# Axial attention with matmuls of 64 and 4 rows on different partitions, and softmax sums normalised inside it

## The chip, the cores and the metric

The kernel runs on one NeuronCore of a Trainium2 chip. The time is that of the whole program on the device, in microseconds (us). The core has a matrix engine (PE; its weight loads are listed apart as PEld), VectorE (DVE), ScalarE (ACT), GpSimd (POOL), and a queue, SP, from which all transfers of this kernel are issued.

## The reference

A trunk of two layers is applied with the same weights to a prompt of 1024 tokens and a sample of 512, all of width 1024. The first, even layer has eight heads of a dilated sliding window beside eight of a latent attention. The second, odd layer is the one that changes:

```
q = rms_norm(q.reshape(B, T, 16, 64), q_norm)        # 16 query heads
k = rms_norm(k.reshape(B, T, 4, 64), k_norm)         # 4 key heads, each for 4 query heads
q, k = axial rope of both (row angles, column angles)
s = einsum(q, k) * 64 ** -0.5                        # dense, per head, prompt and sample apart
p = softmax(s)
o = einsum(p, v)
y = (o * silu(gate)) @ w_out
return x + rms_norm(y, g_post)
```

## The kernel before

Everything is float32. A product of two float32 matrices is made of three matmuls on rounded parts ("hi", and the rest, "lo"): hi x hi, hi x lo, lo x hi. The program runs in phases with a barrier between them: `entry` (projections of layer 0), `attention` of its 16 heads, `output_projection`, `project` (projections of layer 1), `attention` again for the 16 axial heads (tag "c"), `output_projection`. Each engine has its own instruction list, written out in the code's order, and waits on semaphores.

`attention` goes through heads (NH = 16) and ten stages each (NS = 10), g = 10 h + s. Stages 0 and 1 take two of the sample's four key tiles each against its 512 queries, stages 2 to 9 one of the prompt's eight key tiles against 1024 queries. A tile is 128 keys; scores stand transposed, keys on partitions and queries in the free dimension. Per stage:

- PE, `scores` (L1444): for each half x of the score tile SA a matmul of KA (k hi on partitions 0 to 63, k lo on 64 to 127) with Q1 (q hi twice), and one of KB with Q3: 64 rows of k hi with q lo, and 8 rows of ones with rows that hold minus the maximum of each query. So the maximum is already subtracted. The second one has 72 rows.
- ACT: the exponential of SA into PF (L1550), its rounded part PH (L1553; in two stages of ten on DVE, L1657); POOL or DVE: PL = PF - PH (L1689, L1629).
- PE, `pv(g - 3)` (L1484, L1491): six matmuls with V as weights. VH has 64 columns of v and one of ones, so the 65th output row is the sum of the probabilities. They collect in OP (prompt) and OS (sample).
- PE, `max_unit` (L1374): two matmuls of 128 rows give q.k of 128 queries with 512 keys for the next head; DVE takes their maxima (L1601). Once for the sample and once for the prompt of each head a small matmul with the identity transposes the maxima (`transpose_max`, L1387), and DVE multiplies them with a table of minus ones into the rows of Q3 (`augment`, L1619).

After a head's last product ACT copies outputs and sums together (`evac_prompt`, `evac_sample`, L1534, L1543), and SP writes outputs to att_out, sums to att_den. `output_projection` reads the sums, inverts them on DVE (L1943), splits them (L1899, L1945), writes both parts to memory and reads them back as 32 rows (L1795 to L1810). Then per tile of 128 features and 512 tokens the PE spreads them with a matmul of 32 rows (L1864, into rb), DVE multiplies the outputs with it (L1953) and with the gate (L1956), ACT and DVE split them (L1909, L1939). The PE's products (L1877, 24 per output tile) of one third of the tokens run while the next third is prepared.

The score code of the kernel before, for an axial head:

```
for x in range(2):
    out = SA[:, x * CH:(x + 1) * CH]
    q0, k0 = (SEQ, SEQ + (2 * s + x) * P) if s < 2 else (x * CH, (s - 2) * P)
    qs, ks = slice(q0, q0 + CH), slice(k0, k0 + P)
    if stacked[h]:
        mms = [(ka[:, ks], q1[:, qs]), (kb[0:na, ks], q3[0:na, qs])]
    for i, (w, y) in enumerate(mms):
        mm = nc.tensor.matmul(out, w, y, start=(i == 0), stop=(i == len(mms) - 1))
```

## Time and profile before

| | |
|---|---|
| median of 3 runs | 2460.87 us (2458.8 to 2467.92) |
| the profiled execution, its own time | 2463.42 us |
| its span (first to last instruction) | 2461.6 us |
| mean granted TensorE clock | 0.928 of full speed |
| PE busy | 2148.5 us, 87% |
| DVE, POOL, ACT busy | 64%, 46%, 40% |

The span is the time between the first and the last instruction of the program; the execution's own time has a little more around it. A matmul's recorded length is modelled and overlaps with the next one's, so the distance between starts tells more than the length. L and a number is a line of the kernel before; a tile's name is without its buffer number (c_Q is Q1 or Q3).

### The profile page before, as it was taken

What the parts mean: (1) busy time and instruction counts of PE and PEld (TensorE: products, weight loads), DVE (VectorE), ACT (ScalarE), POOL (GpSimd) and SP (SyncE); (2) the same over time, 40 slices, a digit from 0 to 9 for tenths busy, and PEclk for the clock granted to TensorE, in tenths of its full rate; (3) what the DMA queues carried; (4) which work ended last, traced back from release to release, by engine and by line L of the source; (5) the groups of instructions that cost most, each with busy time, mean ns of one, the idle gap of its engine ahead of it and who ended that gap; (6) DMA issues with size and microseconds to landing.
All of it is one profiled execution on the core that took longest, in us unless ns stands there. A gap on an engine that the chain in (4) does not pass through costs nothing. (4 is left out here: it accounts for less than half of the span.)

```text
span 2461.6 us, 25658 instructions
## 1 busy us (share of the span) xinstructions
PE 2148.5 (87%) x9420; PEld 1600.6 (65%) x9420; DVE 1582.5 (64%) x1980; ACT 991.0 (40%) x1259; POOL 1124.1 (46%) x580
## 2 busy tenths in 40 slices
PE   6999988959999999958952987998699999996895
PEld 4777867847777766636742765787466666663674
DVE  7264156756776666625658999995377777773565
ACT  5132133213555566533323232210066666664331
POOL 5333443423555565523126767543266666663300
PEclk9999999977999999978976998999799999998898
DMA  4133487246555554244332222221623232313434
GB/s 154 35 118 129 128 295 192 73 118 126 116 117 112 115 114 99 59 133 140 99 106 83 78 94 98 82 94 65 149 50 82 65 75 65 73 39 112 157 103 128
DMA packets 223272, 262.75 MB, mean 107 GB/s; under 512 B 137440, under 2 KB 147040, under 8 KB 223152
## 3 DMA queue, kind: packets, MB, share of 16 engines
q1 hardware_dynamic: 223152, 261.17, 38.2%
q8 instruction: 72, 1.18, 0.2%
q14 instruction: 48, 0.39, 0.1%
HBM read 162.62 MB, written 98.50 MB: 106 GB/s over the span
## 5 line engine op out<-in xcount | busy, mean ns | idle before, releaser
L1689 POOL TENSOR_TENSOR c_PL<-c_PF,c_PH 128x1024 fp32r<-128x1024 f32 x128 | 307.0, 2399 | 199.1 <-ACT c_PH L1553 142.2
L1689 POOL TENSOR_TENSOR ab_PL<-ab_PF,ab_PH 128x1024 fp32r<-128x1024 f32 (+3 forms) x128 | 269.1, 2102 | 237.1 <-ACT ab_PH L1553 178.8
L1550 ACT ACTIVATE ab_PF<-ab_SA 128x1024 f32<-128x1024 f32 (+3 forms) x160 | 143.6, 897 | 243.6 <-PE ab_SA L1409 143.1
L1550 ACT ACTIVATE c_PF<-c_SA 128x1024 f32<-128x1024 f32 x160 | 164.3, 1027 | 168.7 <-PE c_SA L1444 168.7
L1601 DVE TENSOR_REDUCE c_MH<-c_SM 128x1 f32<-128x512 f32 x256 | 172.9, 688 | 85.2 <-PE c_SM L1374 83.6
L847 PE MATMUL e_acc<-e_XH,e_wh 128*128 128x512 f32 x480 | 197.8, 412 | 25.6 <-DVE e_XL_r L1016 16.1
L340 PE MATMUL p_acc<-XH,p_wh 128*128 128x512 f32 x432 | 186.4, 431 | 26.3 <-POOL Y_r L174 26.3
L847 PE MATMUL e_acc<-e_XL_r,e_wh 128*128 128x512 f32 x480 | 193.5, 403 | 0.0
L847 PE MATMUL e_acc<-e_XH,e_wl 128*128 128x512 f32 x480 | 193.4, 403 | 0.0
L340 PE MATMUL p_acc<-Y_r,p_wh 128*128 128x512 f32 x432 | 172.2, 399 | 0.0
L340 PE MATMUL p_acc<-XH,p_wl 128*128 128x512 f32 x432 | 172.1, 398 | 0.0
L1877 PE MATMUL o_acc<-o_XH,o_WH 128*128 128x512 f32 x384 | 156.6, 408 | 12.4 <-DVE Y_r L1939 12.4
L1877 PE MATMUL o_acc<-o_XH,o_WL_r 128*128 128x512 f32 x384 | 151.2, 394 | 0.0
L1374 PE MATMUL c_SM<-c_KA,c_Q 128*128 128x512 f32 x320 | 132.9, 423 | 20.0 <-DMA c_KA<-kC_lo 18.1
L1553 ACT ACTIVATE c_PH<-c_PF 128x1024 fp32r<-128x1024 f32 x128 | 135.7, 1060 | 4.1
L758 POOL TENSOR_TENSOR e_wl<-e_raw,e_wh 128x1024 fp32r<-128x1024 f32 (+1 forms) x31 | 72.9, 2353 | 135.0 <-ACT e_wh L910 135.0
L1601 DVE TENSOR_REDUCE ab_MH<-ab_SM 128x1 f32<-128x512 f32 x128 | 86.3, 688 | 68.9 <-PE ab_SM L1374 68.6
L1444 PE MATMUL c_SA<-c_Q,c_KA 128*128 128x512 f32 x320 | 127.2, 397 | 1.3 <-ACT c_PF L1550 1.3
L1444 PE MATMUL c_SA<-c_Q,c_KB 72*128 72x512 f32 x320 | 127.2, 398 | 0.0
L847 PEld LDWEIGHTS e_acc<-e_XH,e_wh 128*128 128x128 f32 x480 | 92.6, 193 | 53.3 <-POOL e_wl L758 24.6
L1592 DVE CUSTOM_DVE_ANT_0 ab_BS<-ab_SM,ab_Bhi 128x512 f32<-128x512 f32 (+1 forms) x192 | 83.0, 465 | 66.1 <-PE ab_SM L1370 65.4
L1553 ACT ACTIVATE ab_PH<-ab_PF 128x1024 fp32r<-128x1024 f32 (+3 forms) x128 | 119.6, 934 | 4.1
(255 smaller groups left out, 5569.9 us busy)
## 6 DMA issues: line engine op xcount, KB each, us to landing
o_G<-silu_gate SPq DMA_DIRECT2D x48, 256.0 KB, 2.8
c_Q<-qC_hi SPq DMA_DIRECT2D x32, 384.0 KB, 5.4
e_raw<-in_w_tiles SPq DMA_DIRECT2D x20, 512.0 KB, 3.8
p_raw<-in_w_tiles SPq DMA_DIRECT2D x18, 512.0 KB, 3.6
o_WL<-in_w_out SPq DMA_DIRECT2D x16, 512.0 KB, 5.6
e_XL<-in_xT SPq DMA_DIRECT2D x12, 512.0 KB, 9.8
silu_gate<-e_ta SPq DMA_DIRECT2D x24, 256.0 KB, 2.0
ab_Q<-qA_hi SPq DMA_DIRECT2D x16, 384.0 KB, 5.6
```

The costliest lines, as they stand in the source:

```text
L340: last_mm = nc.tensor.matmul(out, w[:, ks], x[:, k, cols(c)], start=(k == 0 and j == 0), stop=(k == KT - 1 and j == 2))
L758: nc.gpsimd.tensor_tensor(wl[w % 2][:, 0:width], raw[w % 2][:, 0:width], wh[w % 2][:, 0:width].bitcast(F32), ALU.subtract).then_inc(w_lo, 1)
L847: mm = nc.tensor.matmul(out, a[b][:, ks], x[:, k, cols(c)], start=(k + i == 0), stop=(k == KT - 1 and i == 2))
L1374: nc.tensor.matmul(SM[:, x * CH:(x + 1) * CH], Q1[h % 3][0:n, q0:q0 + P], keys(h)[0][0:n, k0:k0 + CH], start=True, stop=True).then_inc(m_r ...
L1444: mm = nc.tensor.matmul(out, w, y, start=(i == 0), stop=(i == len(mms) - 1))
L1550: nc.scalar.activation(used(PF[p], h, s), used(SA, h, s), ACT.Exp).then_inc(e_done, 1)
L1553: nc.scalar.activation(used(PH[p], h, s), used(PF[p], h, s), ACT.Copy).then_inc(p_hi[0], 1)
L1592: nc.vector.tensor_tensor_reduce(out=BS[:, x * CH:x * CH + n], in0=SM[:, x * CH:x * CH + n], in1=table.bitcast(F32), scale=1.0, scalar=-3. ...
L1601: nc.vector.reduce_max(dst, src, axis=AX_X).then_inc(m_done, 1)
L1689: nc.gpsimd.tensor_tensor(used(PL[p], h, s), used(PF[p], h, s), used(PH[p], h, s).bitcast(F32), ALU.subtract).then_inc(p_lo[0], 1)
L1877: mm = nc.tensor.matmul(acc[:, cols(n % NB)], w[:, t, ks], y, start=(k + j == 0), stop=(k == KT - 1 and j == 2))
```

## The change

The axial layer gets its own function `axial`; the even layer keeps `attention`. The order of work over heads and stages stays, with these differences:

- `scores`: KA with Q1 as before, for both halves. The low part of q is now a matmul of 64 rows, on partitions 0 to 63 for the first half and 64 to 127 for the second (KB holds k hi twice, Q3 the two halves of q lo one above the other). The maxima are subtracted by a matmul of their own, of 4 rows: ones on partitions 0 to 3 and, for the prompt's second half, 32 to 35.
- `max_unit` takes 64 rows: even units on partitions 64 to 127, odd ones on 0 to 63. One unit stands behind the scores, the other between the products with PH and those with PL.
- `pv`: VH has 64 columns of v and 64 of ones, so the sum stands in 64 output rows, above the output's partitions. The two VH matmuls come first, then the two with VL, which now has 64 columns.
- ACT makes 1/sum as exp(-ln(sum)) of those rows (`invert`), DVE multiplies the output with it (`normalise`). No sums are written; `output_projection` of layer 1 gets `raw=False` and leaves out everything on the sums, the 24 matmuls of L1864 and the multiplications of L1953. The one of layer 0 keeps them.

```

```diff
+def axial(nc, ar, A, S):
+    NH, NS, NU = 16, 10, 20
+    G = NH * NS
+    NP, NQ = SEQ // P, DEC // P
+    LAG = 3
+    SLOW_HI, SLOW_LO = (3, 5), (4, 8)
...
+        Q1 = [sc.sb(f"c_Q1{i}", [P, T], F32R) for i in range(3)]
+        KA = [sc.sb(f"c_KA{i}", [P, T], F32R) for i in range(2)]
+        KB = [sc.sb(f"c_KB{i}", [P, T], F32R) for i in range(2)]
+        Q3 = [sc.sb(f"c_Q3{i}", [P, 2 * CH], F32R) for i in range(2)]
+        AU = [sc.sb(f"c_AU{i}", [KR, 2 * CH], F32R) for i in range(2)]
+        VH = [sc.sb(f"c_VH{i}", [P, TT, 2 * HD], F32R) for i in range(2)]
+        VL = [sc.sb(f"c_VL{i}", [P, TT, HD], F32R) for i in range(2)]
...
+        RZ = [sc.sb(f"c_RZ{n}", [HD, w]) for n, w in (("s", DEC), ("p", SEQ))]
+        MH = sc.sb("c_MH", [P, NP, 2])
+        M = sc.sb("c_M", [P, 2 * R2 + NQ])
+        one = sc.sb("c_one", [KR, P], F32R)
...
+            def max_unit(h, u):
+                if u == 0:
+                    pe.wait_ge(in_q[h % 3], 32 * (h // 3 + 1))
+                    if h % 4 == 0:
+                        pe.wait_ge(in_k[h // 4 % 2], 32 * (h // 8 + 1))
+                wait_count(pe, m_done, NU * h + u - 1)
+                x, r = u % 2, rows(1 - u % 2)
+                q0, k0 = max_of(u)
+                nc.tensor.matmul(SM[:, half(x)], Q1[h % 3][r, q0:q0 + P], KB[h // 4 % 2][r, k0:k0 + CH],
+                                 start=True, stop=True).then_inc(m_ready, 1)
+            def transpose_max(h, prompt):
+                if prompt:
+                    pe.wait_ge(m_both, h + 1)
+                else:
+                    pe.wait_ge(m_done, NU * h + NQ)
+                wait_count(pe, aug_done, 2 * h + prompt)
+                src = M[:, 0:KR] if prompt else M[:, 2 * R2:2 * R2 + NQ]
+                nc.tensor.matmul(MT[0:KR if prompt else NQ, 0:P], src, ident[:], start=True, stop=True
+                                 ).then_inc(mt_ready, 1)
+            def scores(h, s):
+                q1, q3, au = Q1[h % 3], Q3[h % 2], AU[h % 2]
+                ka, kb = KA[h // 4 % 2], KB[h // 4 % 2]
+                if s == 0:
+                    pe.wait_ge(in_q3[h % 2], 64 * (h // 2 + 1))
+                    if h % 4 == 0:
+                        pe.wait_ge(in_kl[h // 4 % 2], 32 * (h // 8 + 1))
+                wait_count(pe, e_done, h * NS + s)
+                out = [SA[:, half(x)] for x in range(2)]
+                if s < 2:
+                    q0, k0, c, a = (SEQ, SEQ), (SEQ + 2 * s * P, SEQ + (2 * s + 1) * P), half(1), (0, 0)
+                else:
+                    q0, k0, c, a = (0, CH), ((s - 2) * P,) * 2, half(0), (0, R2)
+                for x in range(2):
+                    nc.tensor.matmul(out[x], ka[:, k0[x]:k0[x] + P], q1[:, q0[x]:q0[x] + CH], start=True, stop=False)
+                for x in range(2):
+                    nc.tensor.matmul(out[x], kb[rows(x), k0[x]:k0[x] + P], q3[rows(x), c], start=False, stop=False)
+                if s == 0:
+                    pe.wait_ge(aug_done, 2 * h + 1)
+                if s == 2:
+                    pe.wait_ge(aug_done, 2 * h + 2)
+                for x in range(2):
+                    r = slice(a[x], a[x] + 4)
+                    mm = nc.tensor.matmul(out[x], one[r, :], au[r, c], start=False, stop=True)
+                mm.then_inc(s_ready, 1)
+            def pv(g, between=()):
+                h, s = g // NS, g % NS
+                p, k = g % 4, h // 4
+                vh, vl = VH[k % 2], VL[k % 2]
+                if s == 0:
+                    if h % 4 == 0:
+                        pe.wait_ge(in_v[k % 2], 32 * (k // 2 + 1))
+                    wait_count(pe, o_out[0], h)
+                if s == 2:
+                    wait_count(pe, o_out[1], h)
+                def weighted(t, n, probs, first, last):
+                    for x in range(2):
+                        if s < 2:
+                            out, kt, st, en = OS[0:n, :], NP + 2 * s + x, s == 0 and x == 0, s == 1 and x == 1
+                        else:
+                            out, kt, st, en = OP[0:n, half(x)], s - 2, s == 2, s == NS - 1
+                        mm = nc.tensor.matmul(out, t[:, kt, 0:n], probs[:, half(x)], start=first and st, stop=last and en)
+                    return mm
+                on, n_hi = hi_at[g]
+                pe.wait_ge(p_hi[on], n_hi)
+                weighted(vh, P, PH[p], True, False)
+                weighted(vl, HD, PH[p], False, False)
+                for u in between:
+                    max_unit(h + 1 if s + LAG < NS else h + 2, u)
+                on, n_lo = lo_at[g]
+                pe.wait_ge(p_lo[on], n_lo)
+                weighted(vh, P, PL[p], False, True).then_inc(pv_done, 1)
...
+            for g in range(G):
+                h, s = g // NS, g % NS
+                units = range(2 * s, 2 * s + 2) if h + 1 < NH else ()
+                scores(h, s)
+                for u in units[:1]:
+                    max_unit(h + 1, u)
+                if s == 3 and h + 1 < NH:
+                    transpose_max(h + 1, 0)
+                if g >= LAG:
+                    pv(g - LAG, units[1:])
+                else:
+                    for u in units[1:]:
+                        max_unit(h + 1, u)
+                if s == 0:
+                    transpose_max(h, 1)
...
+            def invert(h, prompt):
+                act.wait_ge(pv_done, NS * h + (NS if prompt else 2))
+                wait_count(act, o_out[prompt], h)
+                src = OP[HD:P, :] if prompt else OS[HD:P, :]
+                nc.scalar.activation(RZ[prompt][:], src, ACT.Ln).then_inc(z_log[prompt], 1)
+                act.wait_ge(z_log[prompt], h + 1)
+                nc.scalar.activation(RZ[prompt][:], RZ[prompt][:], ACT.Exp, scale=-1.0).then_inc(z_inv[prompt], 1)
...
+                if s == 3 and h > 0:
+                    invert(h - 1, 1)
+                if s == 5:
+                    invert(h, 0)
...
+            def both(h):
+                dve.wait_ge(m_done, NU * (h + 1))
+                wait_count(dve, mt_ready, 2 * h)
+                out = M[:, 0:2 * R2].rearrange("p (a b) -> p a b", a=2)[:, :, 0:4]
+                lo, hi = (MH[:, :, j].rearrange("p (a b) -> p a b", a=2) for j in range(2))
+                nc.vector.tensor_tensor(out, lo, hi, ALU.max).then_inc(m_both, 1)
+            def augment(h, prompt):
+                dve.wait_ge(mt_ready, 2 * h + prompt + 1)
+                wait_count(dve, s_ready, NS * (h - 1))
+                n = KR if prompt else 4
+                out = AU[h % 2][0:n, half(1 - prompt)].rearrange("r (i n) -> r i n", n=P)
+                nc.vector.tensor_tensor(out, MT[0:n, 0:P].unsqueeze(1).to_broadcast([n, 4, P]), negsel[0:n, :, :],
+                                        ALU.mult).then_inc(aug_done, 1)
...
+            def normalise(h, prompt):
+                dve.wait_ge(z_inv[prompt], h + 1)
+                wait_count(dve, st[prompt][h % 2], 16 * (h // 2))
+                src = OP[0:HD, :] if prompt else OS[0:HD, :]
+                nc.vector.tensor_tensor(OB[prompt][h % 2][:], src, RZ[prompt][:], ALU.mult).then_inc(o_out[prompt], 1)
...
+                if s == 4 and h > 0:
+                    normalise(h - 1, 1)
+                if s == 6:
+                    normalise(h, 0)
...
+def output_projection(nc, ar, l, S, A, Y, rstd_next, gpost, ones, epst, xin, xout, raw):
...
-            sp.wait_ge(z_hi, 1)
-            sp.dma_start(flat(S["RZ", "hi"]), zh[:].bitcast(F32)).then_inc(z_out, 16)
-            sp.wait_ge(z_lo, 1)
-            sp.dma_start(flat(S["RZ", "lo"]), zl[:].bitcast(F32)).then_inc(z_out, 16)
+            if raw:
+                sp.wait_ge(z_hi, 1)
+                sp.dma_start(flat(S["RZ", "hi"]), zh[:].bitcast(F32)).then_inc(z_out, 16)
+                sp.wait_ge(z_lo, 1)
+                sp.dma_start(flat(S["RZ", "lo"]), zl[:].bitcast(F32)).then_inc(z_out, 16)
...
-            pe.wait_ge(rz_in, 32)
+            if raw:
+                pe.wait_ge(sel_set, 1)
+                pe.wait_ge(rz_in, 32)
             for period, t, g, a, p, x in stages():
-                if g is not None:
+                if g is not None and raw:
                     n = g * KT + t
                     wait_count(pe, o_div, n - 1)
                     nc.tensor.matmul(rb[:, cols(n % 2)], sel[:, t * P:(t + 1) * P], RZ[:, cols(g)], start=True,
...
                         dve.wait_ge(o_in[(0 if t == 0 else 1) if g == 0 else g + 1], 16)
-                    dve.wait_ge(r_ready, n + 1)
-                    nc.vector.tensor_tensor(x_, x_, rb[:, cols(n % 2)], ALU.mult).then_inc(o_div, 1)
-                    dve.wait_ge(o_div, n + 1)
+                    if raw:
+                        dve.wait_ge(r_ready, n + 1)
+                        nc.vector.tensor_tensor(x_, x_, rb[:, cols(n % 2)], ALU.mult).then_inc(o_div, 1)
...
-        attention(nc, ar, "c", A, S, [("c", i, 16 + i) for i in range(16)])
+        axial(nc, ar, A, S)
         with ar.scope() as s1:
-            output_projection(nc, ar, 1, S, A, s1.both("Y1", [P, KT, T]), None, gpost[1], ones, epst, S["X1"], A["yT"])
+            output_projection(nc, ar, 1, S, A, s1.both("Y1", [P, KT, T]), None, gpost[1], ones, epst, S["X1"], A["yT"], False)
...
+    four = np.where(np.arange(36)[:, None] % 32 == np.arange(4)[None, :], -1.0, 0.0).astype(np.float32)
+    c["negsel4"] = np.ascontiguousarray(np.broadcast_to(four[:, :, None], (36, 4, P)))
```

What moves in the PE's list, in a stage of the prompt. c_SA is the score tile, c_SM the one of the maximum units, c_OP the prompt's output, c_one and c_AU the ones and the maxima. Before (65x512 is the output's shape):

```order
L1444 MATMUL c_SA<-c_Q,c_KA 128x512
L1444 MATMUL c_SA<-c_Q,c_KB 128x512
L1444 MATMUL c_SA<-c_Q,c_KA 128x512
L1444 MATMUL c_SA<-c_Q,c_KB 128x512
L1484 MATMUL c_OP<-c_PH,c_VH 65x512
L1484 MATMUL c_OP<-c_PH,c_VL 65x512
L1484 MATMUL c_OP<-c_PH,c_VH 65x512
L1484 MATMUL c_OP<-c_PH,c_VL 65x512
L1374 MATMUL c_SM<-c_KA,c_Q 128x512
L1491 MATMUL c_OP<-c_PL,c_VH 65x512 x2
L1374 MATMUL c_SM<-c_KA,c_Q 128x512
```

The same stage now:

```order
L1865 MATMUL c_SA<-c_Q,c_KA 128x512 x2
L1867 MATMUL c_SA<-c_Q,c_KB 128x512 x2
L1874 MATMUL c_SA<-c_AU,c_one 128x512 x2
L1837 MATMUL c_SM<-c_KB,c_Q 128x512
L1896 MATMUL c_OP<-c_PH,c_VH 128x512 x2
L1896 MATMUL c_OP<-c_PH,c_VL 64x512 x2
L1837 MATMUL c_SM<-c_KB,c_Q 128x512
L1896 MATMUL c_OP<-c_PL,c_VH 128x512 x2
```

Twelve matmuls have become fourteen, and those of one kind stand together: L1865 and L1896 with VH contract over 128 rows, L1867 and L1837 over 64, L1874 over 4; L1896 with VL has 64 output columns.

In ScalarE's list, stages 2 to 5 of a head, c_PF the exponentials, c_PH their rounded part. Before:

```order
L1550 ACTIVATE c_PF<-c_SA 128x1024
L1534 ACTIVATE c_OB<-c_OP 65x1024
L1550 ACTIVATE c_PF<-c_SA 128x1024
L1553 ACTIVATE c_PH<-c_PF 128x1024
L1550 ACTIVATE c_PF<-c_SA 128x1024
L1543 ACTIVATE c_OB<-c_OS 65x512
```

Now:

```order
L1952 ACTIVATE c_PF<-c_SA 128x1024
L1943 ACTIVATE c_RZp<-c_OP 64x1024
L1945 ACTIVATE c_RZp<-c_RZp 64x1024
L1952 ACTIVATE c_PF<-c_SA 128x1024
L1955 ACTIVATE c_PH<-c_PF 128x1024
L1952 ACTIVATE c_PF<-c_SA 128x1024
L1943 ACTIVATE c_RZs<-c_OS 64x512
L1945 ACTIVATE c_RZs<-c_RZs 64x512
```

Where one copy stood there are now two passes over the sums, at the same places between the exponentials.

## Rows read from the trace of the kernel before

**Rows 1.** The page, section 1: the span, busy time, share and instructions per engine.
```profile
span 2461.6 us, 25658 instructions
...
PE 2148.5 (87%) x9420; PEld 1600.6 (65%) x9420; DVE 1582.5 (64%) x1980; ACT 991.0 (40%) x1259; POOL 1124.1 (46%) x580
```

**Rows 2.** Busy time by stretches: engines in us, PEclk the granted clock, then DMA.
```profile
600.00:700.00 100.00, 94.53 (x613) 76.17 (x612) 70.33 (x195) 51.66 (x67) 52.56 (x30) 0.98 0.60 126
1200.00:1300.00 100.00, 66.16 (x272) 50.52 (x270) 59.77 (x67) 28.48 (x50) 26.45 (x19) 0.82 0.36 113
1900.00:2000.00 100.00, 98.84 (x424) 66.23 (x423) 73.62 (x92) 68.63 (x68) 67.16 (x29) 1.00 0.33 74
2300.00:2400.00 100.00, 100.00 (x412) 75.97 (x412) 61.51 (x77) 34.51 (x56) 11.96 (x5) 1.00 0.30 92
```

**Rows 3.** Waits in the odd layer's attention, 1790 to 2240 us: waiter, releaser, us, times, longest.
```profile
ACT c_PF L1550 <- PE c_SA L1444: 134.1, 156, 2.2
```

**Rows 4.** Instructions on the score tile: ns min/median/max, first and last start.
```profile
L1444 PE MATMUL c_SA<-c_Q,c_KA x320: 389/395/628, 1783.8 to 2243.1; 128*128 128x512 f32 x160
```

**Rows 5.** Instructions on the prompt output tile, same columns.
```profile
L1491 PE MATMUL c_OP<-c_PL,c_VH x256: 387/392/402, 1799.8 to 2248.9; 128*65 128x512 f32 x128
```

**Rows 6.** Timeline of the PE, one stage: start, duration, what.
```profile
1975.45 0.39 PE L1374 MATMUL c_SM<-c_KA,c_Q 128*128 128x512 f32 x1
1975.68 0.40 PE L1444 MATMUL c_SA<-c_Q,c_KA 128*128 128x512 f32 x1
...
1978.25 0.40 PE L1374 MATMUL c_SM<-c_KA,c_Q 128*128 128x512 f32 x1
```

**Rows 7.** Timeline of the PE around a transpose of maxima.
```profile
1967.57 0.39 PE L1444 MATMUL c_SA<-c_Q,c_KB 72*128 72x512 f32 x1
1967.89 0.39 PE L1387 MATMUL c_MT<-c_ident,c_M 128*8 128x128 f32 x2
1968.21 0.45 PE L1484 MATMUL c_OS<-c_PH,c_VH 128*65 128x512 f32 x1
1968.49 0.39 PE L1484 MATMUL c_OS<-c_PH,c_VL 128*65 128x512 f32 x1
```

**Rows 8.** Timeline of the PE around a 32-row matmul of the output stage.
```profile
2303.91 0.39 PE L1877 MATMUL o_acc<-Y_r,o_WH 128*128 128x512 f32 x1
2304.14 0.39 PE L1877 MATMUL o_acc<-o_XH,o_WL_r 128*128 128x512 f32 x1
2304.46 0.50 PE L1864 MATMUL o_rb<-o_RZ,o_sel 32*128 32x512 f32 x1
2304.88 0.50 PE L1877 MATMUL o_acc<-o_XH,o_WH 128*128 128x512 f32 x1
2305.22 0.39 PE L1877 MATMUL o_acc<-Y_r,o_WH 128*128 128x512 f32 x1
```

**Rows 9.** Timeline of the PE's weight loads at the same place.
```profile
2303.91 0.19 PEld L1877 LDWEIGHTS o_acc<-o_XH,o_WL_r 128*128 128x128 f32 x1
2304.45 0.18 PEld L1864 LDWEIGHTS o_rb<-o_RZ,o_sel 32*128 32x128 f32 x1 [0.35 <-issue]
2304.88 0.19 PEld L1877 LDWEIGHTS o_acc<-o_XH,o_WH 128*128 128x128 f32 x1 [0.25 <-issue]
```

**Rows 10.** Groups by line, 1900 to 2000 us: busy, mean ns, idle before.
```profile
L1534 ACT ACTIVATE c_OB<-c_OP 65x1024 f32<-65x1024 f32 x4 | 4.0, 1011 | 0.0
```

**Rows 11.** Chain that ended last, 2253 to 2312 us: start, us, what.
```profile
2253.98 1.88 DMA o_z<-att_den
...
2269.30 0.04 DVE Y L1956
...
2290.31 8.13 PE o_acc L1877 x24
```

**Rows 12.** Timeline of the DMA issues at the start of the output stage.
```profile
2254.38 0.43 SPq L1774 DMA_DIRECT2D Y<-att_out  x1
```

**Rows 13.** DMA issues by line, 2245 to 2300 us: count, KB each, us to landing.
```profile
Y<-att_out SPq DMA_DIRECT2D x2, 1024.0 KB, 5.8
```

218 lines of the change are left out of this document (199 added, 19 removed).

## The prediction

> **What bounds the kernel now.** The page first: the PE is busy 87% of the 2461.6 us, more than any other engine [rows 1], so the question is where it is full. The stretches say: in the odd layer's attention 98.84 of 100 us at a granted clock of 1.00, in the output stage 100.00 of 100 [rows 2]. The waits agree: ScalarE waits 134.1 us, 156 times, for the scores, not the PE for ScalarE [rows 3]. So in this attention the PE's queue is the clock of everything. The timeline of one stage (one key tile against all queries of one head) gives its price: from one maximum matmul to the same one a stage later 1975.45 to 1978.25, 2.80 us for 12 matmuls of 512 columns, 0.233 us each, back to back; the second started 0.23 us after the first although each is drawn 0.39 long [rows 6]. The recorded length is thus no price, the distance between starts is. The 160 stages run from 1783.8 [rows 4] to 2249.3 us, the last product's start 2248.9 plus 0.4 [rows 5]: 465.5 us.
>
> **What a change of shape costs.** This is the price the whole sum hangs on. In the output stage a lone matmul of 32 rows stands between matmuls of 128. Undisturbed starts are 0.23 apart (2303.91, 2304.14). Then come 2304.46, 2304.88 and 2305.22 [rows 8]: 1.08 us for three distances that would be 0.69, so 0.39 more for two changes of shape, 0.20 each. The weight loads say why. A load normally runs under the matmul before it: the one of 2303.91 is for the matmul of 2304.14. The 32-row one's load starts at 2304.45, with its own matmul, and so does the next at 2304.88 [rows 8, 9]: at a change of shape the load waits until the stream before has gone by, and is then bare. 0.42 between the two (with a bare 128-column load) against 0.32 before (none) puts the load at 0.10 and the emptying at 0.10. It isn't only rows: the transpose of the maxima has 8 output columns, and from 1967.57 to 1968.49 [rows 7] there are 0.92 us for two slots of 0.233 and two short passes of about 0.11; 0.24 is left for two changes with short loads (8 and 65 columns), 0.12 each.
>
> **The change, part by part.** Per stage the PE now does 2 full matmuls with KA, 2 of 64 rows (low q), 2 of 4 rows (the maxima), one maximum unit of 64 rows, 2 VH, 2 VL with 64 output columns, another maximum unit of 64 rows, 2 VH with the low probabilities: 14 instead of 12, and the shape changes seven times a stage: 128 rows, 64, 32 (4 rows lie in a tile of 32), 64, 128, 128 by 64 columns, 64 rows, 128. Before it changed only around the transposes.
> - Slots: 14 x 0.233 = 3.26.
> - Changes: six with a bare 128-column load, 6 x 0.20, and into VL with half a load 0.15: 1.35.
> - Pairs on different partitions: no row shows two matmuls side by side. Ends: no overlap, 0; complete overlap, one slot of 0.233 per pair. I take that the second needs its own bare load after the first, 0.10, and then streams beside it: it starts 0.10 instead of 0.23 later, 0.13 saved per pair, near the middle. Two pairs: -0.26; in the two sample stages the 4-row matmuls share partitions 0 to 3, one pair: -0.13.
> So a prompt stage costs 4.35, a sample stage 4.48.
> - Transposes: the sample's adds one change (0.10) and 0.22 of passes, 0.32; the prompt's now stands between matmuls of equal shape: 0.10 + 0.03 in, 0.22, 0.20 out, 0.55.
> A head: 8 x 4.35 + 2 x 4.48 + 0.32 + 0.55 = 44.63. Fifteen: 669.5. The last has no maxima ahead: 20 slots (4.66), two changes in each of 10 stages (4.0) and a transpose (0.32) fewer, 35.65. Three closing products, 3 x (6 x 0.233 + 0.15 + 0.20) = 5.25. Together 710.4 against 465.5: +244.9 us.
>
> By the Trainium skill ("TensorE: Matmul & The Clock Gate", Part 3) row-tiled matmuls start about 4 ns apart; no run here shows it, and the sum would be some 29 us lower by it (another 0.10 for each pair), an estimate.
>
> For the changes 64 to 32 and 32 to 64 the nearest row is the 128 to 32 one, 0.20; the ends are 0 and 0.20 [rows 8]. I take 0.20, because rows and columns alike [rows 7, 8] were emptied for. The Trainium skill says it in general ("TensorEngine Tiling (Array Packing)", Key Properties): changing the mode, not merely the tile, drains the engine. The trace agrees for the two modes that it has and shows none of 64 rows.
>
> **Beside the PE.** ScalarE's evacuation (1011 ns for 1024 columns [rows 10]) becomes logarithm and exponential, twice that, and VectorE multiplies once more per part. Cost zero: in 1900 to 2000 us ScalarE has 31 us idle, VectorE 26 [rows 2], and stages get longer. The PE waits for this chain only at the third stage of the products' next head, two stages after it begins; it lasts some 4 us of 8.7. If that cover were gone, under 1 us a head. At the end it is bare: one more pass of ScalarE and a multiplication for one evacuation, +2.3. The loads are the same bytes in other pieces, asked for a head ahead: zero. More ones beside V widen those weight loads from 65 to 128 columns; within a shape they stay under a 0.233 us matmul, as K's do.
>
> **The output stage.** Removed: denominators in, reciprocal, out, and in again, from 2253.98 on, then one 32-row matmul and one multiplication per tile, up to the first product at 2290.31 [rows 11]. Now the first gate multiplication needs only the outputs, issued at 2254.4 and landed 5.8 later [rows 12, 13]: 2260.2 instead of 2269.30 [rows 11]. What follows (21.0 us to the first product) waits for gates that queue behind weights, and I leave it as long: -9.1; ends 0 (the weights' transfers set the end anyway) and -14. In the running part 16 of the 24 selector matmuls stand between full ones, each 0.39 + 0.23: -9.9.
>
> Sum: 244.9 + 2.3 - 9.1 - 9.9 = +228.2. The profiled execution took 2463.4, so 2691.6; the median of the runs is 2.5 below it: 2689 us.
>
> **Rivals.**
> - *Neighbours with fewer than 128 rows change freely.* Then 128 to 64 rows costs, but 64 to 32 to 64 doesn't, and the maximum unit on rows 64 to 127 starts beside the 4-row pair: 0.40 + 0.13 less in 150 stages, a change less in the last 10: -81, 2608 us. For it: rows here show only changes from and to 128. Against: what the array waited for was the shape.
> - *Faster: the changes are free and the pairs complete.* KA 2, low q 1, maxima and the 4-row pair 1, products 6, the second unit 1: 11 slots for 12 in 8 stages of 15 heads, -28, and -16.7 from the ends: 2463.4 - 44.7 - 2.5 = 2416 us. It decides below 44.7 us over 150 x 7 + 10 x 5 = 1100 changes, 0.04 us each; [rows 7, 8] show 0.12 and 0.20. With pairs only as good as I assume, even free changes leave the attention 21 us longer.
> - *The clock falls.* The PE keeps its queue full but streams only about two thirds of the time. In 1200 to 1300 us, busy 66.16%, the granted clock was 0.82; at 600 to 700, with many short matmuls but 94.53 busy, 0.98 [rows 2]. At 0.85 the 3.26 of streaming becomes 3.84, times 155: +90, some 2779 us. Against: those gaps at 1200 were waits of microseconds, these are of 0.2.
> - *The pairs don't overlap.* 8 x 0.26 + 2 x 0.13 = 2.34 more a head: 2726 us; it belongs to the forecast's own range, as does complete overlap (2660).
>
> **How the numbers follow.** The forecast with either kind of pairing 0.62, free neighbours 0.16, falling clock 0.12, the fast case 0.08, something that cancels out 0.02. The likeliest gives 2689. Its own range is 2655 to 2730; to leave out no more than two in ten I reach down to the free neighbours and up to most of the clock's case: 2600 to 2770. Half a per cent (12 us) is about what a measurement of this kernel tells from no change: faster 0.08, same 0.02, slower 0.90.
>
> **What would show it.** Starts in the changed attention: 0.42 to 0.43 us before every matmul that follows a 128-column bare load, seven times a stage; the second of a pair 0.10 after the first (0.23: no overlap; under 0.02: complete); a stage 4.35 long; loads that start with their own matmul. PE granted clock still 1.00. Busy PE stays near 100% though it does less, so the page won't tell. No wait on the normalising multiplication. First output product about 27 us after the attention's stores instead of 36. The prediction is wrong if the shape changes are under 0.1 us, or if the stage is set by a wait for ScalarE or VectorE.

## The result, and where the time is in the changed kernel's profile

| | before | after |
|---|---|---|
| median of the runs, us | 2462.96 | 2648.73 |
| the runs, us | 2458.8, 2460.87, 2465.05, 2467.92 | 2629.85, 2636.07, 2661.38, 2662.24 |
| ratio, 95% interval | | 1.0748 [1.0661, 1.0835] |
| profiled execution, span, us | 2461.6 | 2634.3 |

The changed kernel is 7.5% slower. Its four runs lie further apart than those of before; their mean granted clocks are 0.930, 0.928, 0.919 and 0.918 in the order of the table, so the two longer ones had the lower clock. The stretches and timelines that follow compare the profiled executions (0.928 in both). A run over 1.5% above the fastest of its kernel is left out of a ratio; there is one, of the kernel with the fillers below.

The page of the changed kernel, section 1: busy time and its share, by engine.

```profile
span 2634.3 us, 26268 instructions
...
PE 2328.5 (88%) x9716; PEld 1613.8 (61%) x9716; DVE 1574.4 (60%) x1983; ACT 1021.0 (39%) x1290; POOL 1121.6 (43%) x580
```

Against [rows 1] TensorE has 180 us more "busy" time; ScalarE has 30 us more (two passes over the sums for one copy), VectorE and GpSimd a little less. The page can't say more: time that the changes of shape cost TensorE is drawn as busy. The stretches show that too:

```profile
1900.00:2000.00 100.00, 100.00 (x353) 49.12 (x353) 53.63 (x70) 52.40 (x53) 47.08 (x20) 1.00 0.29 65
2500.00:2600.00 100.00, 100.00 (x440) 82.09 (x439) 53.34 (x68) 30.12 (x51) 3.65 (x2) 1.00 0.29 92
```

The columns are those of [rows 2]. In the odd layer's attention TensorE is full at a granted clock of 1.00, but it gets 353 recorded matmuls into 100 us where it got 424 [rows 2]. The output stage, now without the matmuls of 32 rows, gets 440 (412 before). VectorE and ScalarE fell from 73.6 and 68.6 us to 53.6 and 52.4. Who waits for whom, 1850 to 2400 us:

```profile
ACT c_PF L1952 <- PE c_SA L1874: 249.3, 135, 2.6
...
PEld c_OP L1896 <- issue: 52.1, 216, 0.2
PEld c_SA L1867 <- issue: 48.7, 134, 0.4
PEld c_SM L1837 <- issue: 47.1, 161, 0.4
```

ScalarE's wait for scores was 134.1 us [rows 3]; now 249.3. The last three lines are the new thing: weight loads that start late though no semaphore holds them ("issue"). Another 45.7 us of idle time before loads for c_SM (1841 to 2440 us) are put down to VectorE's maxima. But those units start 0.32 to 0.33 us behind the product before them in every case, as do the ones without such a wait: nothing waits there beyond the change of shape. One stage on TensorE, to set beside [rows 6]:

```profile
2101.03 0.63 PE L1865 MATMUL c_SA<-c_Q,c_KA 128*128 128x512 f32 x2
2101.58 0.51 PE L1867 MATMUL c_SA<-c_Q,c_KB 64*128 64x512 f32 x2
2102.02 0.50 PE L1874 MATMUL c_SA<-c_AU,c_one 4*128 4x512 f32 x2
2102.45 0.50 PE L1837 MATMUL c_SM<-c_KB,c_Q 64*128 64x512 f32 x1
2102.87 0.73 PE L1896 MATMUL c_OP<-c_PH,c_VH 128*128 128x512 f32 x2
2103.45 0.62 PE L1896 MATMUL c_OP<-c_PH,c_VL 128*64 128x512 f32 x2
2104.00 0.49 PE L1837 MATMUL c_SM<-c_KB,c_Q 64*128 64x512 f32 x1
2104.42 0.73 PE L1896 MATMUL c_OP<-c_PL,c_VH 128*128 128x512 f32 x2
2104.99 0.39 PE L1865 MATMUL c_SA<-c_Q,c_KA 128*128 128x512 f32 x1
```

A stage lasts 2104.99 - 2101.03 = 3.96 us where it lasted 2.80 [rows 6]. Read the starts: a lone matmul of 64 rows is followed 0.42 us later by the next one (2102.45 to 2102.87), 0.19 more than the 0.233 of matmuls of one shape. The low-q pair (2101.58) and the pair of 4 rows (2102.02) take 0.44 and 0.43 for two matmuls each: taken apart, the second of either pair starts 3 ns (median) after the first, which by itself says only that they start together; whether they also share their time is asked below.

The two spans differ by 172.7 us. Where these are; the pieces end at the first start on the score tile, the last product's end, the first start on o_acc behind it, and the span's end:

| piece | before | after | difference | forecast |
|---|---|---|---|---|
| up to the attention's first score matmul | 1783.8 | 1786.3 | +2.5 | 0 |
| the odd layer's attention | 465.5 | 651.5 | +186.0 | +244.9 |
| from its end to the first output product | 41.0 | 35.05 | -6.0 | +2.3 - 9.1 |
| output stage | 171.3 | 161.5 | -9.8 | -9.9 |
| sum | | | +172.7 | +228.2 |

From the changed kernel's trace: instructions on the score tile, the output stage's first load of outputs, and the end of the chain in front of the first product.

```profile
L1865 PE MATMUL c_SA<-c_Q,c_KA x320: 388/397/796, 1786.3 to 2430.8; 128*128 128x512 f32 x160
```

```profile
2444.61 0.38 SPq L2129 DMA_DIRECT2D Y<-att_out  x1
```

```profile
2468.80 2.62 DVE Y L2319
...
2472.85 2.50 PE o_acc L2237 x5
```

From that load to the first product it was 35.9 us [rows 11, 12] and is 28.2 (forecast 27): the round trip of the denominators is gone. The chain in front of the first product now consists of gate transfers (o_G) for the most part.

### The profile page after: what moved, and what is told of

Read it like the earlier page. It is cut to its first block and busy times, and to the rows that moved or that the text cites. A ratio compares the mean times of both kernels' runs of the same rounds, so it can differ in the third digit from the quotient of the medians.

```text
span 2634.3 us, 26268 instructions
## 1 busy us (share of the span) xinstructions
PE 2328.5 (88%) x9716; PEld 1613.8 (61%) x9716; DVE 1574.4 (60%) x1983; ACT 1021.0 (39%) x1290; POOL 1121.6 (43%) x580
## 5 line engine op out<-in xcount | busy, mean ns | idle before, releaser
L1952 ACT ACTIVATE c_PF<-c_SA 128x1024 f32<-128x1024 f32 x160 | 164.0, 1025 | 318.3 <-PE c_SA L1874 318.3
L1550 ACT ACTIVATE ab_PF<-ab_SA 128x1024 f32<-128x1024 f32 (+3 forms) x160 | 143.6, 897 | 246.4 <-PE ab_SA L1409 145.8
L2237 PE MATMUL o_acc<-o_XH,o_WH 128*128 128x512 f32 x384 | 155.0, 404 | 41.5 <-DVE Y_r L2300 41.5
L1837 PE MATMUL c_SM<-c_KB,c_Q 64*128 64x512 f32 x320 | 161.0, 520 | 21.4 <-DMA c_negsel<-in_negsel 18.7
L2237 PE MATMUL o_acc<-o_XH,o_WL_r 128*128 128x512 f32 x384 | 151.0, 393 | 0.0
L1837 PEld LDWEIGHTS c_SM<-c_KB,c_Q 64*128 64x128 f32 x320 | 59.9, 192 | 131.3 <-issue 53.7
L1955 ACT ACTIVATE c_PH<-c_PF 128x1024 fp32r<-128x1024 f32 x128 | 135.5, 1059 | 4.1
L1553 ACT ACTIVATE ab_PH<-ab_PF 128x1024 fp32r<-128x1024 f32 (+3 forms) x128 | 119.6, 934 | 4.1
L340 PEld LDWEIGHTS p_acc<-XH,p_wh 128*128 128x128 f32 x432 | 84.2, 195 | 54.0 <-issue 36.9
```

The source lines that it names most:

```text
L340: last_mm = nc.tensor.matmul(out, w[:, ks], x[:, k, cols(c)], start=(k == 0 and j == 0), stop=(k == KT - 1 and j == 2))
L1550: nc.scalar.activation(used(PF[p], h, s), used(SA, h, s), ACT.Exp).then_inc(e_done, 1)
L1553: nc.scalar.activation(used(PH[p], h, s), used(PF[p], h, s), ACT.Copy).then_inc(p_hi[0], 1)
L1837: nc.tensor.matmul(SM[:, half(x)], Q1[h % 3][r, q0:q0 + P], KB[h // 4 % 2][r, k0:k0 + CH], start=True, stop=True).then_inc(m_ready, 1)
L1952: nc.scalar.activation(PF[p][:], SA[:], ACT.Exp).then_inc(e_done, 1)
L1955: nc.scalar.activation(PH[p][:], PF[p][:], ACT.Copy).then_inc(p_hi[0], 1)
```

## The experiments

**One part alone: the normalising.** Before's matmuls all stay; only the sums get 64 rows and are inverted and applied inside the last attention.

```diff
...
-    nc.tensor.matmul(out, w[:, kt, 0:HD + 1], PH[p][:, pc], ...)
+    n = 2 * HD if norm and i == 0 else HD + 1
+    nc.tensor.matmul(out[0:n, :], w[:, kt, 0:n], PH[p][:, pc], ...)
...
+                if norm and s == 4 and h > 0:
+                    normalise(h - 1, 1)
```

> Kernel before, with one part of the change alone: VH with 64 columns of ones, 1/sum as exp(-ln(sum)) on ScalarE and the multiplication on VectorE inside the axial attention, and layer 1's output stage without the sums. Scores, maxima units and order of the products as before, all matmuls in the 128-row shape. My theory (the whole loss is the shape changes on the PE, the normalisation a gain): attention stage stays 2.80 us, +2.3 us after the last product, first output product 27 us after the attention instead of 36 and 16 selector matmuls of 0.62 less: about 2463 - 17 = 2446 us (2438 to 2452). Rival (the wider VH weights or the longer ScalarE and VectorE chain cost in the attention): the stage grows to 2.9 to 3.0 and the time comes out at 2460 to 2480.

Measured: 2457.82 us (10 runs), ratio 0.9974 [0.996, 0.9987]. That is neither the 2446 of the theory nor the longer stages of the rival. In the profile the output stage is 11 us shorter and the transition ahead of it 7, but the attention took 10 more (first to last score matmul 469.4 in place of 459.3). With stages of 2.8 us the cover that I had counted on in the changed kernel is not there. Timeline of TensorE in this kernel:

```profile
1978.58 0.39 PE L1451 MATMUL c_SA<-c_Q,c_KB 72*128 72x512 f32 x1
1979.25 0.50 PE L1492 MATMUL c_OP<-c_PH,c_VH 128*128 128x512 f32 x1 [0.28 <-DVE c_OB L1660]
```

Once a head the start comes 0.67 us after the last and not 0.23, behind VectorE's product (L1660). That product stood behind the maxima of stage 4. So it was moved ahead of them:

```diff
+                if norm and s == 4 and h > 0:
+                    normalise(h - 1, 1)
                 for u in units[:some]:
                     maximum(h + 1, u)
-                if norm and s == 4 and h > 0:
-                    normalise(h - 1, 1)
```

> The kernel before with all its narrow matmuls kept; only the normalising is moved into the last attention, as in the first such kernel of this study, but on VectorE the division of head h-1's prompt half is placed ahead of the maximum unit of stage 4 and not behind it. Theory: what was lost there (a head of the attention 0.67 us longer, 10 us in all, TensorE waiting some 0.43 us once a head for the division before it may write OP again) was VectorE's order alone. Then the wait goes, the attention lasts about 460 us (first run of this form 469.4, before 459.3 between the same two points), and the time is 2447 to 2452. Rival: what TensorE waits for is the logarithm and exponential on ScalarE, whose place is unchanged: then the same 2457.8.

Measured: 2451.21 us (6 runs), ratio 0.9954 [0.9936, 0.9971]. All that TensorE's own records wait for between 1841 and 2250 us in this kernel is

```profile
PE c_MT L1394 <- DVE c_M L1634: 4.4, 14, 0.5
PE c_SA L1451 <- ACT c_PF L1573: 0.6, 1, 0.6
```

and the first of the two is in the kernel before as well (4.3). A head is back from 29.80 to 29.29 us (29.18 before). The theory holds, and this half of the change is a gain of half a per cent.

**The low-q pair on the same partitions.** The changed kernel, with both matmuls reading rows 0 to 63.

```diff
-   nc.tensor.matmul(out[x], kb[rows(x), ...], q3[rows(x), c], start=False, stop=False)
+   nc.tensor.matmul(out[x], kb[rows(0), ...], q3[rows(0), c], start=False, stop=False)
```

> Changed kernel, but both low-q matmuls of a stage use partitions 0 to 63 (so the second half of the queries gets the low part of the first half: that part of the scores is wrong). Nothing else moves. My theory (two matmuls on different partitions stream at the same time, starts 3 ns apart in the changed kernel's trace): the second starts 0.23 us after the first, the stage grows from 3.96 to 4.19, 160 stages +37 us, about 2673 us with the clock as in the profiled run of the changed kernel. Rival (the two starts are only drawn together and the array does them one after the other): no change, 2636.

Measured: 2666.96, one run; span 30.9 us longer than the changed kernel's. The pair's row:

```profile
2101.20 0.73 PE L1867 MATMUL c_SA<-c_Q,c_KB 64*128 64x512 f32 x2
2101.86 0.49 PE L1874 MATMUL c_SA<-c_AU,c_one 4*128 4x512 f32 x2
```

0.66 us where 0.44 stood. 160 times 0.22 would be 35 us, and the attention alone is 36.8 us longer (688.3 for 651.5); the span grew less because the attention began 5.4 us earlier, behind code that is the same in both. The pairs are real.

**The maxima subtracted with 64 rows.** The changed kernel with R2 = 64: one and AU have 128 rows, 60 of each 64 hold zeros. Low-q products, subtraction and the maximum unit behind them then have one shape, and two of the six changes of a stage go.

```diff
-    R2 = 32
+    R2 = 64
...
-                    r = slice(a[x], a[x] + 4)
+                    r = slice(a[x], a[x] + 64)
```

> Changed kernel, but the maxima are subtracted by matmuls of 64 rows (4 with data, 60 of zeros) instead of 4, on partitions 0 to 63 and 64 to 127; in the two sample stages both low-q and both maxima matmuls stand on 0 to 63. So low-q, maxima and the unit behind them have one shape, two changes of shape fewer in a stage. My theory (a change between 64 and 32 rows costs as much as one from 128, 0.20): a prompt stage 3.96 - 0.40 = 3.56 us, a sample stage 3.56 + 0.23 (its low-q pair no longer side by side), total about 2636 - 0.4 x 150 - 0.2 x 10 + 7 = 2581 us. Rival (neighbours with fewer than 128 rows change for nothing): 3.96, no gain, 2636 to 2643.

Measured: 2570.18, one run. One stage:

```profile
2101.47 0.62 PE L1865 MATMUL c_SA<-c_Q,c_KA 128*128 128x512 f32 x2
2102.02 0.51 PE L1868 MATMUL c_SA<-c_Q,c_KB 64*128 64x512 f32 x2
2102.36 0.40 PE L1875 MATMUL c_SA<-c_AU,c_one 64*128 64x512 f32 x2
2102.60 0.39 PE L1837 MATMUL c_SM<-c_KB,c_Q 64*128 64x512 f32 x1
2102.93 0.73 PE L1897 MATMUL c_OP<-c_PH,c_VH 128*128 128x512 f32 x2
```

From the low-q pair to the next 0.34 (0.44 in the changed kernel), from the subtraction to the maximum unit 0.24 (0.43). So a change between 64 and 32 rows did cost, and the rival in which such neighbours are free falls. The stage is 3.57 us for 3.96, 0.20 for each of the two changes. Zeros multiplied are cheaper than a change of shape.

The whole time is 11 us below the forecast of 2581. Its + 7, for the low-q products that share partitions in the sample stages, was not paid. A sample stage of this kernel:

```profile
1936.32 0.50 PE L1868 MATMUL c_SA<-c_Q,c_KB 64*128 64x512 f32 x1
1936.33 0.50 PE L1837 MATMUL c_SM<-c_KB,c_Q 64*128 64x512 f32 x1
1936.66 0.39 PE L1868 MATMUL c_SA<-c_Q,c_KB 64*128 64x512 f32 x1
1936.89 0.63 PE L1875 MATMUL c_SA<-c_AU,c_one 64*128 64x512 f32 x2
```

The maximum unit (c_SM, partitions 64 to 127) stands in TensorE's list behind both low-q products and both subtractions, all on 0 to 63. It starts 0.01 us after the first of them, ahead of the other three, in all 30 such stages: five matmuls take four slots.

**Both maximum units behind the low-q pair.** They are a pair on different partitions too, and a stage has three changes of rows for six.

```diff
                 for x in range(2):
                     nc.tensor.matmul(out[x], kb[rows(x), ...], q3[rows(x), c], ...)
+                for u in units:
+                    max_unit(h + 1, u)
...
-                scores(h, s)
-                for u in units[:1]:
-                    max_unit(h + 1, u)
+                scores(h, s, units)
```

> The changed kernel, with both maximum units of a stage issued directly behind the pair of low-q matmuls, as a pair on different partitions, and the pair of subtracted maxima behind them. Theory (a change of tile shape costs 0.19 us, pairs overlap completely): a stage has 11 matmul times of 0.233 and three changes (128 to 64 rows, 64 to 32, 32 to 128), 2.56 + 0.58 = 3.15 us in place of 3.96, so about 120 us less than 2636: 2515 (2505 to 2530). Rival, the cost goes by the pieces of narrow work and not by changes of shape (0.19 for each group of narrow matmuls wherever it stands): six groups become three as well, but a change from 64 to 32 rows would be free (the profile had 0.43 there), 2.95 and 2485. Rival, VectorE is late: the maxima of a stage come together and are read one after the other, so that TensorE waits for them: 3.6 us or more, 2580.

Measured: 2537.03, one run. The stages are as forecast:

```profile
2104.83 0.63 PE L1865 MATMUL c_SA<-c_Q,c_KA 128*128 128x512 f32 x2
2105.39 0.51 PE L1867 MATMUL c_SA<-c_Q,c_KB 64*128 64x512 f32 x2
2105.72 0.40 PE L1837 MATMUL c_SM<-c_KB,c_Q 64*128 64x512 f32 x2
2106.05 0.49 PE L1876 MATMUL c_SA<-c_AU,c_one 4*128 4x512 f32 x2
2106.47 0.72 PE L1898 MATMUL c_OP<-c_PH,c_VH 128*128 128x512 f32 x2
...
2107.97 0.63 PE L1865 MATMUL c_SA<-c_Q,c_KA 128*128 128x512 f32 x2
```

3.14 us. But stage 5 of each head (by the starts of ScalarE's exponentials) takes 3.97, and stage 3 takes 4.20, of which some 0.3 are the transpose there. That is 1.6 us a head, 24 in all, for the 22 by which the kernel misses its forecast. The same grouping with the 64-row subtraction has two changes:

> As the grouped kernel, but the maxima are subtracted with matmuls of 64 rows of which 60 hold zeros, so that low-q products, maximum units and subtraction have one shape. (In the sample stages both low-q products and both subtractions stand on the same partitions, one after the other.) Theory: 11 matmul times and two changes a stage, 2.56 + 0.39 = 2.95 us: 2570 - 0.57 x 150 = 2485 (2475 to 2500). That is still more than the 2.80 us of a stage before, since two changes cost more than the one matmul time that each pair saves in twice: the kernel stays slower than before. Rival: with one shape for the whole group the load of the next weights is hidden and a change costs under 0.1: 2.75 us, 2455.

Measured: 2510.18, one run. Two starts of the same matmul:

```profile
2105.97 0.62 PE L1865 MATMUL c_SA<-c_Q,c_KA 128*128 128x512 f32 x2
...
2108.92 0.40 PE L1865 MATMUL c_SA<-c_Q,c_KA 128*128 128x512 f32 x1
```

An undisturbed stage is 2.95 us, as forecast; the 25 us above the forecast are again stages 3 and 5 (4.22 and 3.77). So with six, four, three and two changes a stage, what is left beyond its slots of 0.233 is 1.16, 0.77, 0.58 and 0.39 us: 0.19 a change each time. Even undisturbed it would be longer than before's 2.80: a group of narrow matmuls costs 0.39 in all, and its pairs save one slot of 0.233 against the kernel before.

What stages 3 and 5 wait for was asked by putting the division behind both maxima of stage 4 and not between them.

```diff
-                for u in units[:1]:
-                    maximum(h + 1, u)
+                for u in units:
+                    maximum(h + 1, u)
                 if s == 4 and h > 0:
                     normalise(h - 1, 1)
...
-                for u in units[1:]:
-                    maximum(h + 1, u)
```

> The grouped kernel (both maximum units behind the low-q pair) with VectorE's two maxima of a stage one directly behind the other and the division (normalising) behind both, not between them. In the grouped kernel stage 5 of each head took 3.97 us where its neighbours took 3.14, the second maximum unit starting 0.6 us late. Theory: it waits for the maximum that stands behind the division of stage 4; then stage 5 falls to 3.15 to 3.4 and the time from 2537 by 8 to 12 us to 2525 to 2529. Rival: stage 5 is long for VectorE's whole load around stage 4 (the augmented rows, the copy and the subtraction of other stages), then 3.9 and 2537 again.

Measured: 2537.37, one run, stage 5 again 3.97: the theory falls. Its timeline, from the start of stage 3's maximum units on, shows what it is (PE, its weight loads and DVE):

```profile
2108.27 0.39 PE L1837 MATMUL c_SM<-c_KB,c_Q 64*128 64x512 f32 x2
...
2110.19 0.93 DVE L2023 CAST c_PH<-c_PF 128x1024 fp32r<-128x1024 f32 x1 [3.34 <-ACT c_PF L1949]
...
2111.03 1.28 DVE L1975 TENSOR_REDUCE c_MH<-c_SM 128x1 f32<-128x512 f32 x2
...
2111.77 0.18 PEld L1837 LDWEIGHTS c_SM<-c_KB,c_Q 64*128 64x128 f32 x1 [0.22 <-DVE c_MH L1975]
...
2112.36 0.18 PEld L1837 LDWEIGHTS c_SM<-c_KB,c_Q 64*128 64x128 f32 x1 [0.41 <-DVE c_MH L1975]
```

The maxima of stage 3 were ready to be read at 2108.7, but in stages 3 and 5 VectorE has the copy of the probabilities ahead of them, and VectorE stands idle for 3.34 us until that stage's exponential is there. The next stage's second unit waits for the maximum of this one's (the last line). Grouping brought the second unit of every stage forward and left VectorE's order where it was. Maxima ahead of the copy in those stages should mend it; that was not run, so this cause is read from the timeline and not tested.

**64 columns for the low values, in the kernel before.** It asks for the price of the change of columns alone, 128 to 64.

```diff
+   n = HD if i == 1 and h >= NA and shared else HD + 1
+   nc.tensor.matmul(out[0:n, :], w[:, kt, 0:n], PH[p][:, pc], ...)
```

> Kernel before, but in the axial attention the VL products take 64 columns of weights instead of 65 (the 65th was zero), so they have the 128 by 64 shape, and since VH and VL alternate the shape changes four times a stage (more at the sample's). If a change of columns costs like one of rows, less the shorter load (0.15 and 0.20): +0.7 us a stage, +112 us, about 2575. If a change of columns from 128 to 64 is free, as the 0.23 us between VH and VL in the changed kernel's trace say: within 0.5% of before, 2455 to 2470. I expect the second.

Measured: 2462.64, ratio 0.9991 [0.9977, 1.0005]: free.

**128 columns for the transposes, in the kernel before**, the other end of it. Only the last attention's 32 are padded; the first keeps its 8 columns.

```diff
+   MW = AUG if NA else P        # NA = 0 in the last attention alone
...
-   nc.tensor.matmul(MT[0:AUG, 0:P], M[:, c:c + AUG], ident[:], ...)
+   nc.tensor.matmul(MT[0:MW, 0:P], M[:, c:c + MW], ident[:], ...)
```

> The kernel before, with the maxima's transposes padded to 128 columns of M, so that their stationary operand has the 128x128 shape of all others (before it has 128x8). It asks what the 0.09 us is that a transpose costs beyond its own time at each end. Theory, it goes by the number of columns: then the start after a 32-column-group operand costs nothing any more, and from the matmul ahead of the transpose to the transpose stand 0.23 us in place of 0.32, 64 heads' transposes in all, 5 us less: 2456. Rival, it goes by the type (F32 there, F32R elsewhere): the same 0.32 and the same 2461.

Measured: 2463.87, one run. TensorE's timeline, beside [rows 7]:

```profile
1968.17 0.39 PE L1445 MATMUL c_SA<-c_Q,c_KB 72*128 72x512 f32 x1
1968.40 0.38 PE L1388 MATMUL c_MT<-c_ident,c_M 128*128 128x128 f32 x2
1968.54 0.48 PE L1485 MATMUL c_OS<-c_PH,c_VH 128*65 128x512 f32 x1
1968.86 0.39 PE L1485 MATMUL c_OS<-c_PH,c_VL 128*65 128x512 f32 x1
```

0.69 us where [rows 7] have 0.92: a stationary operand (the one that is loaded) of 8 columns does cost two changes, and padding it with 120 useless columns is quicker. This is the sample's transpose; by the medians of the stages it gave 0.22 us and the prompt's 0.10. First to last score matmul took 454.8 us for 459.3. The expectation had counted 64 transposes, and 32 were padded. The whole run didn't get shorter in this one execution: its attention began 2.3 us later, and the transition behind took 43.5 us for 41.0.

**TensorE kept occupied ahead of the attention.** In the changed kernel the full clock comes back 20 us later than before.

```diff
             for u in range(NQ):
                 max_unit(0, u)
+                filler()      # two matmuls of 64 rows into OS, not yet in use
...
```

> The changed kernel with two more matmuls of 64 rows (into OS, which nobody has yet written) behind each of head 0's maximum units, ahead of the first scores; results unchanged. Theory: in the changed kernel TensorE's clock is at half from 1756 to 1807 us (before: 1753 to 1787) because TensorE stood idle between head 0's maximum units and the stream after them is broken at each change; with TensorE kept occupied there, full clock comes at about 1787 and the time falls by 4 to 9 us, 2640 in the median of runs against 2649, and the runs lie closer together (they spread from 2630 to 2662). Rival: the late rise has nothing to do with what TensorE does in head 0's maxima; then the fillers cost what they take, 0 to +5 us, and the clock rises at 1807 as before.

Measured: 2643.9 us (4 runs: 2637.22, 2640.5, 2647.3 and 2694.86), ratio 1.0735 [1.0704, 1.0765], not to be told from the changed kernel's 1.0748. The time alone decides nothing, since it lies near the theory's 2640; the clock does. The stretches of the kernel with the fillers and then of the changed kernel, columns as in [rows 2]:

```profile
1753.00:1787.00 34.00, 24.17 (x66) 17.62 (x66) 15.46 (x24) 0.23 (x1) 0.00 (x0) 0.50 0.82 174
1787.00:1804.00 17.00, 16.22 (x38) 6.59 (x36) 5.75 (x9) 7.26 (x7) 8.94 (x4) 0.50 0.00 1
```

```profile
1753.00:1787.00 34.00, 13.85 (x24) 5.70 (x24) 15.54 (x26) 1.67 (x2) 0.00 (x0) 0.54 0.92 196
1787.00:1804.00 17.00, 16.22 (x39) 6.59 (x37) 6.02 (x11) 7.26 (x7) 7.91 (x4) 0.50 0.00 0
1812.00:1829.00 17.00, 17.00 (x62) 8.59 (x61) 8.42 (x12) 9.54 (x11) 7.12 (x3) 1.00 0.03 8
```

TensorE was busy 24.2 us for 13.9 ahead of the attention (17.1 in the kernel before), and the clock still rose at 1805.4. The theory falls as far as these fillers test it; they leave TensorE idle for 10 of the 34 us. The attention is as long as without them (651.3 us). The cause of the late rise is not found. What the runs show is that it comes with the changed attention: 51 to 58 us at half clock at this place in each of the seven traces with the function `axial`, 34 in each of the seven with the old one; the clock rises 20 to 23 us after the first score matmul, not 2 to 4. Which part of `axial` does it is not separated; the form with two changes a stage has it too (54.6 us). Some 17 us more at half of 2.4 GHz are about 9 us of the 186.

**The version that the runs point to.** Normalising inside both attentions and no selector matmuls in either output stage, from the second kernel above:

```diff
-  attention(nc, ar, "ab", A, S, [...])
+  attention(nc, ar, "ab", A, S, [...], True)
...
-  output_projection(nc, ar, 0, ..., S["X1"], True)
+  output_projection(nc, ar, 0, ..., S["X1"], False)
```

> The faster kernel of this study (before, with the normalising of the last attention moved into it) with the same done in the first attention: 64 columns of ones in the high values, the logarithm and exponential on ScalarE, the product on VectorE, and no selector matmuls and reciprocals in layer 0's output stage either. Theory: layer 0's output stage loses what layer 1's lost (171.3 to 161.5, 9.8 us), and the first attention, whose stages in the window heads are heavier on TensorE for each score tile, hides the chain as the last one does: 2441 (2437 to 2446). Rival: in the first attention VectorE also forms biases and reads maxima with a table, so the product comes late there and TensorE waits for OP once a head, 0.4 to 1 us x 16: 2447 to 2458.

Measured: 2441.89 (5 runs), ratio 0.9906 [0.9889, 0.9922]. Then with the transposes of both attentions padded to 128 columns:

```diff
-   nc.tensor.matmul(MT[0:AUG, 0:P], M[:, c:c + AUG], ident[:], ...)
+   nc.tensor.matmul(MT[:, 0:P], M[:, c:c + P], ident[:], ...)
```

> The fastest kernel of this study (both attentions normalise their own outputs, all narrow matmuls as before) with the maxima's transposes padded to 128 columns in both attentions. Theory: the padding took 4.4 us out of the last attention in the profile of the kernel before (first to last c_SA<-KA start 454.8 in place of 459.3), and about as much in the first, 32 transposes each; the time is 2442 - 5 to 9 = 2435 (2432 to 2438). Rival: what the attention gives back is lost in the transition behind it, since the padded kernel before ran in 2462.1 as the kernel before does: 2441 to 2442.

Measured: **2428.99 us** (5 runs, 2420.2 to 2429.64), ratio to the kernel before **0.9849 [0.9824, 0.9874]**, more than forecast. Its score matmuls in the last attention:

```profile
L1451 PE MATMUL c_SA<-c_Q,c_KA x320: 387/395/628, 1761.6 to 2218.3; 128*128 128x512 f32 x160
```

456.7 us, 4.9 less than without the padding (461.6); and they begin 13.5 us earlier than there (1775.1). Of these 6.8 are the first attention's, from its first score matmul to its last product (505.1 us for 511.9). The profile compared is 20.7 us shorter, and the two attentions give 11.7 of them. Of the rest, 2.4 stand ahead of the first attention, 4.3 between the two and 3.1 behind the last, where the edit changes nothing; by such amounts the traces differ in code that they share (5.4 above). The medians' 12.9 us is the better measure, though two of the five runs are 8 us below the other three.

## Why the prediction was right, and which terms were off

Forecast 2689, measured 2648.7 (profile 2636): slower by the mechanism named. Step by step:

- *What bounds it.* Right: TensorE's queue is the clock of everything in this attention, after as before, and nobody else's lighter work shows in the time.
- *The price of a change of shape.* Right. Six changes cost 3.96 - 12 x 0.233 = 1.16 us a stage, 0.193 each; taken from [rows 8] it was 0.20. By the medians a change costs 0.09 ahead of the first matmul of the new shape and 0.10 behind it, in either direction (in the 64-row kernel 64 rows after 128: 0.327, then 0.340 to the next of 64; 128 after 64: 0.323, then 0.337). The recorded loads agree with the reading as an emptying and a bare load: at a change the load starts with its own matmul and the next load 0.11 us later. Six changes at 0.007 less are some 7 us.
- *The change into VL.* Wrong term: counted as a seventh change, 0.15 a stage. It costs nothing (VH to VL has the starts of one shape, and 64 columns alone left the kernel before at 0.9991). 24 us. The prediction had carried the price of the transposes' 8 columns over to 64; the two are not alike, as the padded transposes confirm.
- *The pairs.* Wrong term: 0.13 saved per pair, between two ends; it is the whole slot, 0.233. Two pairs, 0.20 a stage, 29 us over the attention. The Trainium skill had it right ("TensorE: Matmul & The Clock Gate", Part 3): about 4 ns between row-tiled matmuls, measured 3. Its sum was the closer one.
- *Sum of a stage.* 4.35 forecast, 3.96 measured; a head 44.63, measured 40.93 (medians of the ten stages, by ScalarE's exponentials). Times 15, 55 of the 58.9 us by which the attention was overestimated.
- *The ends of the attention.* A slip of the sum: it adds three closing products (5.25 us) to 16 heads with ten products each, but the first three stages of head 0 have none, and the closing ones are these. The last head was also put some 5 us too long. These 10 us and the late clock, which works the other way, about cancel; that the 15 heads seem to explain nearly all of the error is partly luck. The changes counted for a whole attention come to 220 us, so that with free ones it would be 25 longer than before by the prediction's own terms, not 21; nothing hangs on it.
- *Beside the TensorE.* Right at zero: the trace of the changed kernel has no wait of TensorE, or of its weight loads, for the normalising. The condition ("two stages after it begins", with long stages) was needed: at 2.8 us the same chain cost 0.43 us a head until VectorE's order was changed.
- *Transition and output stage.* -6.0 for -6.8, and -9.8 for -9.9.
- *The clock.* 1.00 in the attention's body, as said, against the rival of 0.85. Not foreseen: the late rise at its start, some 9 us, with the opposite sign to the other errors, and the wider spread of the runs.

The Trainium skill's rule that a change of mode empties the engine ("TensorEngine Tiling (Array Packing)", Key Properties) agrees with these traces for rows, 128 to 64 and 64 to 32 (0.19 us a change), and for 8 columns against 128; for 64 columns against 128 they show no cost (0.9991), and the measurement decides.

Of the rivals, free neighbours falls by the 64-row subtraction (0.39 us less a stage for two changes fewer, 0.20 each); the fast case needed 0.04 us a change and there are 0.19, though its pairs were complete; pairs that don't overlap falls, complete overlap (2660, inside the forecast's own range) is what happened.

## What to carry to other kernels

Count changes of tile shape along TensorE's queue, not useful rows: here one costs 0.19 us, nearly a matmul of 512 columns (0.233), so narrow matmuls on different partitions pay only in groups in which they save more than the two changes around them, 0.39 us. Padding with zeros to the neighbours' shape was cheaper than the narrow shape in both cases tried (64 rows for 4; 128 columns for 8). And test the parts of a change apart: here the normalising, done in both attentions, was worth nearly a per cent, while the narrow matmuls cost eight.

## What was not expected of the hardware

- Two matmuls of 64 rows on different partitions start 3 ns apart and cost one slot; on the same partitions 0.22 us more.
- A matmul on free partitions started ahead of three others that stand before it in TensorE's list on the other half (30 of 30 sample stages of the 64-row kernel).
- 128 against 64 output columns costs nothing, 128 against 8 costs 0.22 us for the pair of changes around the sample's transpose and 0.10 around the prompt's.
- Behind the first matmul after a change the next of the same shape starts 0.34 us later, not 0.233, pair or not (the 64-row stage above, 2102.02 to 2102.36); behind the second pair it is 0.24 again (2102.36 to 2102.60), so the pair itself adds nothing.
- With the new attention the granted clock stayed at half 17 to 24 us longer around its start than with the old one, with 13.9 as with 24.2 us of matmuls in the 34 us ahead of it.
